# A weight ring of seven places in a two-layer trunk kernel, with eight small loads moved from GpSimd's DMA queue to ScalarE's

## The reference, cut to what matters

```python
def hier_moe(h, wg, bg, we, be, w1, w3, w2):
    t = h.reshape(-1, D)
    ...                                    # group and expert probabilities, top 2 experts: gate
    for e in range(MOE_EXPERTS):           # 32
        he = jax.nn.silu(t @ w1[e]) * (t @ w3[e])       # (1024, 512) twice
        y = y + gate[:, e:e + 1] * (he @ w2[e])         # (512, 1024)
    return y

for layer in range(2):
    x = x + mixer(rmsnorm(x, mix_norm[layer]))
    x = x + hier_moe(rmsnorm(x, ffn_norm[layer]), ...)
```

## Time and profile before

| what | value |
|---|---|
| time, median of 3 runs | 1420.05 us (1419.77 to 1421.86) |
| the profiled execution, its own time | 1420.41 us |
| its span | 1418.6 us |
| mean granted TensorE clock | 0.931 |
| PE busy | 1156.8 us (82%) |
| DVE, ACT, POOL busy | 371.0, 264.8, 26.5 us |
| read from HBM | 451.97 MB, 319 GB/s over the span |

### The profile page before, as it was taken

How to read it: one execution, slowest core, us unless ns; L and a number is a source line. 1 busy time by engine, 2 the same in 40 slices (tenths; PEclk the granted TensorE clock), 3 DMA queues, 4 the chain that set the end, 5 groups by cost and what they waited for, 6 DMA issues and landing times.

```text
span 1418.6 us, 20352 instructions
## 1 busy us (share of the span) xinstructions
PE 1156.8 (82%) x8298; PEld 645.1 (45%) x8298; DVE 371.0 (26%) x933; ACT 264.8 (19%) x485; POOL 26.5 (2%) x36
## 2 busy tenths in 40 slices
PE   4998797977869778686899999979886787868777
PEld 2665654433334233342587776454442334424232
DVE  2346623101101011110555653251111111101111
ACT  2224322101111011110233444030110101101010
POOL 1012100000000000000000000000000000000000
PEclk9999898998989899998999999979999989989989
DMA  9720074999999999999852235419999999999994
GB/s 313 264 101 1 33 323 173 421 421 422 422 423 422 422 422 422 422 422 419 287 204 97 104 119 224 179 72 388 421 422 423 422 422 422 422 422 423 422 422 207
DMA packets 80111, 453.51 MB, mean 320 GB/s; under 512 B 10393, under 2 KB 10637, under 8 KB 30925
## 3 DMA queue, kind: packets, MB, share of 16 engines
q1 hardware_dynamic: 78556, 452.10, 78.3%
q0 software_dynamic: 288, 0.33, 0.2%
q10 hardware_dynamic: 1232, 0.62, 0.2%
HBM read 451.97 MB, written 1.05 MB: 319 GB/s over the span
## 4 chain that ended last, share of the span: by engine, by line
PE 59%; DMA 27%; DVE 6%; issue 3%; SPq 3%; ACT 2%; ACTq 0%; DVEq 0%
DMA ring<-in_moe_w 26%; PE bank L694 13%; PE bank L664 10%; PE bank L734 9%; PE bank L684 5%; PE bank L645 4%; PE bank L444 4%; PE bank L848 4%; SPq L329 2%; PE bank L594 2%; PE bank L654 1%; PE bank L452 1%; PE bank L805 1%; DMA vrow<-in_od_conv_b 1%; DVE ys L1514 1%
## 5 line engine op out<-in xcount | busy, mean ns | idle before, releaser
L664 PE MATMUL bank<-ring,xT 128*32 128x256 f32 x4096 | 285.5, 429 | 153.0 <-DMA ring<-in_moe_w 139.2
L664 PEld LDWEIGHTS bank<-ring,xT 128*32 128x32 f32 x4096 | 137.1, 117 | 302.2 <-DMA ring<-in_moe_w 160.2
L694 PE MATMUL bank<-ys,pgT 128*128 128x512 f32 x512 | 236.4, 604 | 14.0 <-DVE ys L1514 14.0
L694 PEld LDWEIGHTS bank<-ys,pgT 128*128 128x128 f32 x512 | 92.0, 189 | 153.7 <-issue 125.6
L734 PE MATMUL bank<-h,ring 128*128 128x256 f32 x576 | 130.4, 382 | 0.0
L1042 ACT ACTIVATE ys<-bank 128x512 f32<-128x512 f32 x64 | 38.3, 598 | 477.5 <-PE bank L684 477.5
L734 PEld LDWEIGHTS bank<-h,ring 128*128 128x128 f32 x576 | 107.3, 190 | 18.6 <-issue 5.1
L1508 DVE COPY heT<-bank 128x128 f32<-128x128 f32 x64 | 18.7, 292 | 299.1 <-PE bank L672 299.1
L1504 DVE TENSOR_TENSOR he<-sg,bank 128x128 f32<-128x128 f32 x64 | 18.4, 288 | 261.3 <-ACT sg L1036 261.3
L1514 DVE COPY ys<-bank 128x512 f32<-128x512 f32 x64 | 44.3, 692 | 136.7 <-PE bank L684 136.7
L684 PE MATMUL bank<-extra,heT 128*32 128x512 f32 x512 | 63.3, 611 | 14.5 <-DVE heT L1508 7.6
(11 more groups left out here) (301 smaller groups left out, 929.2 us busy)
## 6 DMA issues: line engine op xcount, KB each, us to landing
ring<-in_moe_w SPq DMA_DIRECT2D x320, 1024.0 KB, 21.7
extra<-in_moe_w SPq DMA_DIRECT2D x64, 1024.0 KB, 24.5
ring<-in_od_w_in SPq DMA_DIRECT2D x20, 1024.0 KB, 9.4
ring<-in_ev_w_in SPq DMA_DIRECT2D x12, 1024.0 KB, 12.7
ring<-in_od_w_out SPq DMA_DIRECT2D x8, 1024.0 KB, 6.0
ring<-in_ev_w_out SPq DMA_DIRECT2D x4, 1024.0 KB, 9.5
x<-in_x SPq DMA_DIRECT2D x2, 512.0 KB, 6.3
out<-x SPq DMA_DIRECT2D x2, 512.0 KB, 2.7
```

Source lines behind the costliest of these rows:

```text
L664: last = mm(bank[4 + e % 2][32 * j:32 * j + 32, 0:256], xT[:, 4 * part + k, CAP * e:CAP * e + CAP], w[:, k, :, 256 * (j // 2) + j % 2:256 ...
L694: last = mm(bank[2 * t + h][:, :], pgT[:, e, t, :], ys[:, e % 2, 512 * h:512 * h + 512], start=False, stop=False)
```

## The change

The ring has seven places, so that with the two extra ones nine units can be held. The room comes from `vrow`, which now lies in a buffer that is used later, and from the memory kept for the descriptors of POOL's DMAs, which is set to 1024 bytes. Three pairs of units share a place, (0,0) with (2,0), (0,1) with (2,1), (1,0) with (3,0); (1,1) and (3,1) get places of their own. Nine units of the first expert step are issued before any unit that needs the expert stage to run: (3,1) moves up in `FIRST`. In the mixers unit v waits for unit v-7. The eight router loads go from POOL to ACT, behind ACT's four loads and ahead of `norm_root(0)`.

```diff
-RING = 6
+RING = 7
+SWDGE_BYTES = 1024
-FIRST = [(0, 0), (0, 1), (0, 2), (1, 2), (1, 0), (1, 1), (2, 2), (3, 2), (2, 0), (2, 1), (3, 0), (3, 1)]
+FIRST = [(0, 0), (0, 1), (0, 2), (1, 2), (1, 0), (1, 1), (2, 2), (3, 1), (3, 2), (2, 0), (2, 1), (3, 0)]
+PLACES = {(0, 0): 0, (2, 0): 0, (0, 1): 1, (2, 1): 1, (1, 0): 2, (3, 0): 2, (1, 1): 3, (2, 2): 4, (3, 1): 5, (3, 2): 6,
+          (0, 2): RING, (1, 2): RING + 1}
+SHARED = {(0, 0): (2, 0), (0, 1): (2, 1), (1, 0): (3, 0), (2, 0): (0, 0), (2, 1): (0, 1), (3, 0): (1, 0)}
 def slot_of(layer, unit):
-    return (unit + 3 * layer) % RING
+    return (unit + MIX_UNITS[0] * layer) % RING
-        vrow = sb("vrow", [96, 256])
+        vrow = gg[0:96, 0, 0:256]
...
-                        sp.wait_ge(used[0], last_step * STEP_UNITS + finished(*((2, 0), (2, 1), (3, 0), (3, 1), (2, 2), (3, 2))[v]))
+                        sp.wait_ge(used[0], last_step * STEP_UNITS + finished(*((2, 0), (2, 1), (3, 0), (1, 1), (2, 2), (3, 1), (3, 2))[v]))
...
                 for e, part in FIRST:
+                    place = PLACES[e, part]
+                    if (e, part) in SHARED and e >= 2:
+                        sp.wait_ge(used[layer], finished(*SHARED[e, part]))
+                    elif place < RING - 1:
+                        sp.wait_ge(*emptied(layer, MIX_UNITS[layer] - RING + place))
+                    elif place == RING - 1:
+                        sp.wait_ge(*((mo_acc[0], NT), (o_ps, 8))[layer])
                     else:
+                        sp.wait_ge(*(((on_ok, 1), (on_ok, 1)), ((lm_ok, SSM_H), (sq_in, 16)))[layer][place - RING])
...
-                            if part < 2 and e >= 2:
-                                sp.wait_ge(used[layer], (i + 1) * STEP_UNITS + finished(e - 2, part))
+                            if (e, part) in SHARED and e >= 2:
+                                sp.wait_ge(used[layer], (i + 1) * STEP_UNITS + finished(*SHARED[e, part]))
                             else:
-                                sp.wait_ge(used[layer], i * STEP_UNITS + finished(e + 2 if part < 2 else e, part))
+                                sp.wait_ge(used[layer], i * STEP_UNITS + finished(*SHARED.get((e, part), (e, part))))
...
             act.dma_start(qkn[:, 1, :], A["at_k_norm"].to_broadcast([P, 64])).then_inc(in_even, 16)
+            for l in range(2):
+                act.dma_start(wr[:, l, :, 0:4], A["moe_wg"][l].rearrange("(k p) n -> p k n", p=P)).then_inc(in_small, 16)
+                act.dma_start(wr[:, l, :, 4:36], A["moe_we"][l].rearrange("(k p) n -> p k n", p=P)).then_inc(in_small, 16)
+                act.dma_start(br[:, l, 0:4], A["moe_bg"][l:l + 1, :].to_broadcast([P, 4])).then_inc(in_rb, 16)
+                act.dma_start(br[:, l, 4:36], A["moe_be"][l:l + 1, :].to_broadcast([P, 32])).then_inc(in_rb, 16)
...
-            for l in range(2):
-                pool.dma_start(wr[:, l, :, 0:4], A["moe_wg"][l].rearrange("(k p) n -> p k n", p=P)).then_inc(in_small, 16)
-                pool.dma_start(wr[:, l, :, 4:36], A["moe_we"][l].rearrange("(k p) n -> p k n", p=P)).then_inc(in_small, 16)
-                pool.dma_start(br[:, l, 0:4], A["moe_bg"][l:l + 1, :].to_broadcast([P, 4])).then_inc(in_rb, 16)
-                pool.dma_start(br[:, l, 4:36], A["moe_be"][l:l + 1, :].to_broadcast([P, 32])).then_inc(in_rb, 16)
...
-    nc = bacc.Bacc("TRN2", target_bir_lowering=False, num_devices=1)
+    nc = bacc.Bacc("TRN2", target_bir_lowering=False, num_devices=1, dynamic_dma_scratch_size=SWDGE_BYTES)
```

More of the change, by code:

```diff
@@ L305, in moe_slot @@
         def moe_slot(layer, e, part):
-            if part == 2 and e < 2:
-                return RING + e
-            return slot_of(layer, MIX_UNITS[layer] + ((2 * e + part) % 4 if part < 2 else 2 + e))
+            place = PLACES[e, part]
+            return place if place >= RING else slot_of(layer, MIX_UNITS[layer] + place)
         def moe_memory(layer, e, part):
@@ L318, in moe_full @@
             before = sum(slot_of(layer, v) == slot for v in range(MIX_UNITS[layer]))
-            turn = (2 * e + part) // 4 if part < 2 else 0
-            return 32 * (before + turn + 1), 64 if part < 2 else 32
+            both = (e, part) in SHARED
+            return 32 * (before + 1 + (both and e >= 2)), 64 if both else 32
         block = ctx.enter_context(nc.Block())
@@ L380, in _ @@
                 for e, part in FIRST:
[L381 to L390, removed]
+                    place = PLACES[e, part]
+                    if (e, part) in SHARED and e >= 2:
[4 more added lines that the diff above has]
+                        sp.wait_ge(*((mo_acc[0], NT), (o_ps, 8))[layer])
                     else:
-                        sp.wait_ge(*((mo_acc[0], NT), (o_ps, 8))[layer])
+                        sp.wait_ge(*(((on_ok, 1), (on_ok, 1)), ((lm_ok, SSM_H), (sq_in, 16)))[layer][place - RING])
                     moe_unit(layer, e, part, e)
```

## The result

The changed kernel takes 1422.72 us (median of 20 runs, 1420.77 to 1426.04), the kernel before 1420.45 (20 runs, 1418.76 to 1422.77). The ratio is 1.0014, with a 95% interval of 1.0008 to 1.0021: 2.0 us slower, between 1.1 and 3.0 (2.3 by the medians). That is inside the 0.2% which I had called no change. Forecast were 1426.3, 6.3 slower. The profiled execution has a span of 1419.8 us, 1.2 more than before.

A forecast was written before the change was run, and what follows sets the result against it. Loads bound the expert stages; the ScalarE and VectorE chain bounds the first 23 us. Ninth unit -8.1, ACT's late start +14.4, sum +6.3 us: 1426.3 us against 1420.05, own range 1424 to 1429, with rival (a) 1411 to 1430.

The forecast's parts named there:

- rival (b): At the start, ACT is held only in part, 5 to 9 us net; time near 1420, within 1417 to 1421; chance 0.14.
- Together -8.1 us: Both layers' expert stages: the ninth unit loaded ahead saves 4.2 and 3.9 us, together 7.6 to 8.6.
- The dry moments: Before the second (2,0) of each expert stage SP's load queue runs empty, 0.5 to 1.0 and 0.8 to 1.3 us.
- The step of 59.6 us: Later expert steps of 12 units keep their length of 59.6 us; costed at nothing.
- its queue takes only so many packets: At the start, a full queue holds up an engine's DMA issue; SP had about 1,720 packets waiting.
- Packet by packet, whatever the size: At the start, queues alternate single packets, so ACT's tiny packets go one for each of SP's 2 KB packets.
- The level sums of 5 us: Earlier trace, 5 to 10 us: q1 moved 311 packets, q10 294, taken as evidence for turns one for one.
- rival (a): At the start, ACT isn't held and the router loads cost nothing: 1411.9 us; chance 0.20.
- ACT is free at 23.6 to 25.1; I take 24.2: At the start, the time in us when ACT's eight router load issues are all put in and it can go on.
- +14.4: At the start, ACT's late first activation delays VectorE's copy from 17.61 to 32.0 us, 14.4 us lost (12.7 to 16.4).
- ACT's 3,720th then goes when SP's does, at 24.9 us now: At the start, ACT goes on once 3,720 packets have moved, at the pace of SP's queue, before two corrections.
- The room in the queue: Packets that may wait in a DMA queue, about 1,720 by SP's count, assumed for ACT's queue too.

The follow-up runs named there:

- e10: Kernel before (six places), router loads issued late by SP, and (3,0) loaded ahead of (2,2) in the steps after the first: 1409.19 us.
- e7: Changed kernel, router loads issued late by SP, and (3,0) loaded ahead of (2,2) in the steps after the first: 1401.81 us.
- e6: Changed kernel, router loads issued late by SP, and (2,2) loaded ahead of (2,0) in the steps after the first: 1407.85 us.
- e4: Changed kernel, ACT's eight loads bring the same bytes in 128 pieces each, true router loads issued late by SP: 1410.22 us, one execution.
- e5: Changed kernel, SP holds its unit loads back until the eight router loads have landed: 1415.23 us, one execution.
- e9: Changed kernel, SP's seven vector loads of `vrow` issued behind the first seven units: 1444.76 us, one execution.
- e1: Also e1_late: changed kernel, the eight router loads taken from ACT and issued by SP just ahead of unit (0,2) of layer 0: 1410.06 us.
- e3: Kernel before (six places), router loads taken from POOL and issued by SP late in layer 0's mixer: 1415.90 us.
- e8: Changed kernel, router loads left on POOL, each weight load cut into two of 64 partitions to fit 1 KB for descriptors: 1409.51 us.

## Why the prediction had the sign and not the size

The time lay in my range, between the forecast and rival (b), in the band of no change to which I had given 0.09. Nearest to what happened is rival (b), to which I had given 0.14: ACT held only in part, 5 to 9 us net, since its queue drains faster while SP's small packets pass. The start cost 8.3 in this way.

**Right: a unit in hand for a unit less to wait for.** "Together -8.1 us" measured -7.2 in the traces, 7.4 between e10 and e7. The dry moments were 4.97 - 3.85 = 1.1 and 4.97 - 3.31 = 1.7 us by these sums, where I had said 0.5 to 1.0 and 0.8 to 1.3. In layer 0 the second (2,0) was issued at 287.08, as late as the whole stage, but its first half landed 5.5 us after that, not 4.7 to 5.2. In layer 1 it landed in 5.2, but was issued at 1010.74, which is 4.85 later than before where the stage's first `up` is 4.50 later. The sizes were off a little, and the mechanism holds, since e6 took the dips away and its stages are 0.6 and 0.9 us shorter.

**Right: nothing else moved.** The step of 59.6 us, the mixers and the tail were costed at nothing, and the start (+8.2) and the stages (-7.2) make up the change of span to 0.2 us.

**Right: ACT is held by its full queue, and takes turns packet by packet.** e4 (pieces, not loads or bytes), e5 (no turns, 959 packets a us) and e9 (1049 to 1050) show each half. The counting holds too: q10 moved 5,440 packets in all in the changed kernel and 1,856 in e4, as reckoned, each piece a packet and 16 more a load. SP's queue moved 9,756 up to 150 us, which are 9,268 pieces, 16 for each of 25 loads and 88 for the seven of `vrow`; so up to 30.19 it is 312 beside the pieces, where I had some 310.

That "its queue takes only so many packets" shows at SP as well. Its first load of `vrow`, 16 pieces, takes 0.67 us to issue in the changed kernel, where fewer than 500 packets had been put in, and 4.89 in e9 (one execution), where it stands behind fourteen halves of a unit, with 7,824 packets put in and 5,366 moved, so some 2,460 waiting. The kernel before had 1,325 to 1,896 waiting when the issue of a half ended, from the third half to the twelfth, counted in the way that gave 1,720 for the eleventh. These are the measured counts; a fixed number of packets is not shown.

"Packet by packet, whatever the size" is shown for q1 and q10 and for the sizes that they had here. With units of 2 KB pieces in q1 it is 1033 to 1028 packets from 18 to 24 us. From 15 to 17 us q1's packets have only 580 bytes in the mean (it loads pieces of 272), and both go faster and stay level, 877 to 900. In e9 it is 1232 to 1235 from 14 to 17 us, at 570 bytes. The stretch in which it fails, 8 to 11 us, stands under "Wrong" below.

The queues of the changed kernel from 19.0 to 19.1 us:

```profile
q1 hardware_dynamic: 16, 0.03, 92.1%
q10 hardware_dynamic: 17, 0.00, 12.7%
```

Over the 45 stretches of 0.1 us from 19.0 to 23.5 us it is 14 to 20 packets of q1 and 15 to 21 of q10, about one of each for every one of the 16 engines. One is a piece of 2 KB, which takes an engine 94 ns (median), the other one of 16 or 128 bytes. Turns of several packets would show there, as I estimate from these figures: eight pieces of 2 KB in a row are 0.75 us of an engine (8 x 94 ns), in which it would move nothing of q10, and counts over 0.1 us would scatter far more than 14 to 21. The level sums of 5 us, which I had held against rival (a), don't decide it: turns of equal length on both sides would keep such sums level too.

**Wrong: "ACT is free at 23.6 to 25.1; I take 24.2".** Measured were 18.31, and this term alone made +14.4 of what was +8.3. The failing step is "ACT's 3,720th then goes when SP's does, at 24.9 us now". It takes the turns as one for one from the first packet on. They were so from 11 to 24 us (2,966 packets of q1, 2,976 of q10), but from 8 to 11 us q1 moved 489 packets and q10 1,528. That SP's queue then served the seven loads of `vrow` is what e9 tested: with them moved behind the units, the queues were level in that stretch too and ACT was free at 24.51. I had taken the rule from the earlier trace rows, where the queues look level in just those microseconds. The queues of the kernel before from 8 to 11 us:

```profile
q0 software_dynamic: 145, 0.18, 55.6%
q1 hardware_dynamic: 173, 0.44, 48.3%
q10 hardware_dynamic: 182, 0.02, 6.0%
```

POOL's queue has over half of the engines' time there, and each queue moves no more than some 60 packets a us. With POOL's loads gone, ACT's queue moved 509 a us. That it was POOL's packets which had kept it level is argued from these rows and wasn't tried. Nor was it taken apart why SP's queue falls behind while it serves these small loads.

The room in the queue was mis-sized as well. When ACT's last issue ended at 18.31, q10 had moved 3,921 of 5,440 packets, so some 1,520 were waiting and not 1,720. These 200 are 1.2 us of hold more; the 1,039 packets ahead, 6.1 us less, outweigh them. In e9 it was 1,660. The room is therefore no fixed number of packets when counted in this way.

**Left out: the vector rows.** I had kept the wait for `vrow` as a cover of 3.9 us that hides part of ACT's delay, and counted POOL's freed loads at nothing. In fact `vrow` landed at 11.35 as soon as POOL's loads were gone. In the changed kernel this didn't show, as ACT was later than either. In e1 and e3 it is a gain of 4.2 and 4.4 us at the projection, and e3, which has nothing else, is 5.1 us faster. The profile before had it on show, as the wait of 3.91 in the earlier trace rows.

**Open** is why the first products of the projection run at half the pace in some executions (e1_late, e4, e7, e8, e9) and not in the others, when TensorE comes to them from the same 16 transposes and some 1 us of idling in e1_late as in e3.

## What to carry to other kernels

Before a load is moved to another engine's queue, count its pieces, not its bytes: 4,608 pieces of 16 and 128 bytes kept ScalarE issuing until 18.3 us, the same bytes in 1,024 pieces until 7.1. As these two queues took turns one packet each (1033 to 1028 in 6 us), small pieces in one went at the pace of the big ones in the other, so place them where the other queue is idle or nobody stands behind them. And here the prefetch brought most of what the profile promised (7.2 to 7.4 us of 8.1): the loss lay in what was moved to make room for it.

## What the runs showed of the hardware that was not expected

- ScalarE's and SyncE's queues took turns one packet for one, with pieces of 2 KB against 16 and 128 bytes: 688 to 689 (11 to 15 us), 1033 to 1028 (18 to 24 us) and, in e9, 1049 to 1050. With nothing beside it, ScalarE's queue moved 959 a us.
- While SyncE's queue served seven small loads it fell behind: 489 packets to the other's 1,528 in 3 us; with these loads moved away (e9, one execution) it was 319 to 324.
- ScalarE stopped within its DMA instruction, here four times for 2.7 to 3.8 us, and was let go for good with some 1,520 of its packets waiting (1,660 in e9). A load of 128 pieces stood for the 1,024 of the load ahead of it.
- With 249 packets of POOL's queue in the first 12 us the small loads of SP's queue came 5.6 us later (TensorE's first use of `vrow` was at 17.04, and at 11.35 and 11.45 in the changed kernel and e8).
- With 1 KB for descriptors POOL waited 4.2 to 6.2 us before seven of its eight weight loads (e8), and this did good, as its loads no longer came all at once.
- The first products of a phase ran at half the pace in some executions: 853 ns a product in place of 429 in e1_late, 5.30 us for 16 in place of 3.69 in e6, there with a granted clock of 0.72.
